# Column products with the high and low parts of the moving operand side by side, and a VectorE sum of the two halves

## The reference

```python
# first block
for i in (0, 1):
    mix = dsa_mixer(h, ...) if i == 0 else gla_mixer(h, ...)
    h = layer_norm(ALPHA * h + mix)
    h = layer_norm(ALPHA * h + square(relu(h @ w_up)) @ w_down)      # w_up 1024 x 4096
# second block
for i in (0, 1):
    mix = mla_mixer(h, ...) if i == 0 else hgrn2_mixer(h, ...)
    h = layer_norm(ALPHA * h + mix)
    gate, up = h @ w_in                                             # 1024 x 2 * 2816
    h = layer_norm(ALPHA * h + (silu(gate) * up) @ w_down)
    h = h + sigmoid(h @ w_ple_gate) * (p @ w_ple_proj)
```

## Time and profile before

| | |
|---|---|
| Median of 3 runs | 1422.44 us (1420.7 to 1422.44) |
| Profiled execution, its own time | 1421.68 us |
| Its span in the profile | 1419.9 us |
| TensorE busy with products | 1311.9 us (92%) |
| VectorE busy | 843.4 us (59%) |
| ScalarE busy | 572.2 us (40%) |
| Mean granted TensorE clock | 0.967 of full |

### The profile page before, as it was taken

How to read it: one execution, slowest core, us unless ns; L and a number is a source line. 1 busy time by engine, 2 the same in 40 slices (tenths; PEclk the granted TensorE clock), 3 DMA queues, 4 the chain that set the end, 5 groups by cost and what they waited for, 6 DMA issues and landing times.

```text
span 1419.9 us, 19097 instructions
## 1 busy us (share of the span) xinstructions
PE 1311.9 (92%) x8181; PEld 1185.4 (83%) x8181; DVE 843.4 (59%) x1146; ACT 572.2 (40%) x652; POOL 82.6 (6%) x198
## 2 busy tenths in 40 slices
PE   6978899997998899999878899999999988999997
PEld 5867799996987799997767899998898877999996
DVE  5584855557566755557645754447667658554465
ACT  5452344443633344443342433444451233433333
POOL 2450000000000000000230000000000000000000
PEclk9999999999999999999889999999999999999999
DMA  7410655554632455554330655555553325555542
GB/s 247 147 60 2 207 178 185 198 181 145 189 129 90 156 197 181 185 198 144 119 119 8 226 190 178 185 195 191 172 164 119 119 67 178 180 192 192 179 152 86
DMA packets 128757, 221.06 MB, mean 156 GB/s; under 512 B 6904, under 2 KB 97040, under 8 KB 128672
## 3 DMA queue, kind: packets, MB, share of 16 engines
q1 hardware_dynamic: 125648, 209.83, 44.1%
q0 software_dynamic: 3024, 10.01, 2.4%
HBM read 218.77 MB, written 1.05 MB: 155 GB/s over the span
## 4 chain that ended last, share of the span: by engine, by line
PE 80%; DVE 12%; ACT 4%; DMA 3%; issue 1%; POOL 0%; SPq 0%; ACTq 0%; POOLq 0%
PE ps L499 18%; PE ps L476 18%; PE ps L477 18%; PE ps L478 17%; PE ps L745 2%; DVE wlo L1354 2%; PE ps L584 2%; DVE y L1429 2%; DVE stats L1400 1%; PE ps L597 1%; DVE y L1397 1%; DVE x L1432 1%; ACT whi L1008 1%; ACT buf L1076 1%; PE ps L713 1%
## 5 line engine op out<-in xcount | busy, mean ns | idle before, releaser
L1354 DVE TENSOR_TENSOR wlo<-raw,whi 128x2048 fp32r<-128x2048 f32 (+2 forms) x201 | 454.0, 2265 | 259.1 <-ACT whi L1008 258.8
L1008 ACT ACTIVATE whi<-raw 128x2048 fp32r<-128x2048 f32 (+2 forms) x201 | 377.9, 1886 | 172.2 <-DMA raw<-in_mlp_w_down 46.5
L476 PE MATMUL ps<-xh,whi 128*128 128x256 f32 x1400 | 398.5, 285 | 6.1 <-ACT buf L1270 2.4
L477 PE MATMUL ps<-xh,wlo 128*128 128x256 f32 x1400 | 397.9, 284 | 0.0
L478 PE MATMUL ps<-xl,whi 128*128 128x256 f32 x1400 | 397.7, 284 | 0.0
L476 PEld LDWEIGHTS ps<-xh,whi 128*128 128x128 f32 x1400 | 270.3, 193 | 9.3 <-issue 5.0
L477 PEld LDWEIGHTS ps<-xh,wlo 128*128 128x128 f32 x1400 | 270.3, 193 | 1.6
L478 PEld LDWEIGHTS ps<-xl,whi 128*128 128x128 f32 x1400 | 270.2, 193 | 0.0
L476 PE MATMUL ps<-whi,hh 128*128 128x512 f32 x432 | 168.7, 390 | 0.0
L477 PE MATMUL ps<-whi,hl 128*128 128x512 f32 x432 | 168.6, 390 | 0.0
L478 PE MATMUL ps<-wlo,hh 128*128 128x512 f32 x432 | 168.1, 389 | 0.0
(11 more groups left out here) (281 smaller groups left out, 1101.8 us busy)
## 6 DMA issues: line engine op xcount, KB each, us to landing
raw<-in_ffn_w_in SPq DMA_DIRECT2D x44, 1024.0 KB, 5.1
raw<-in_mlp_w_up SPq DMA_DIRECT2D x32, 1024.0 KB, 5.4
raw<-in_mlp_w_down SPq DMA_DIRECT2D x32, 1024.0 KB, 4.9
raw<-in_ffn_w_down SPq DMA_DIRECT2D x22, 1024.0 KB, 4.8
raw<-in_hgrn_w_in SPq DMA_DIRECT2D x16, 1024.0 KB, 5.4
raw<-in_b_w_in SPq DMA_DIRECT2D x12, 1024.0 KB, 5.3
raw<-in_a_w_in SPq DMA_DIRECT2D x8, 1024.0 KB, 7.2
raw<-in_ple_w_gate SPq DMA_DIRECT2D x8, 1024.0 KB, 6.0
```

What stands on the lines that cost most here:

```text
L476: mm(o, a[0], b[0], start=start, stop=False)
L477: mm(o, a[1], b[0], start=False, stop=False)
L1008: a.activation(whi[:, slot, 0:w], raw[:, slot, 0:w], ACT.Copy).then_inc(s["hi_done"], 1)
L1354: v.tensor_tensor(wlo[:, slot, 0:w], raw[:, slot, 0:w], whi[:, slot, 0:w].bitcast(F32), ALU.subtract).then_inc(s["lo_done"], 1)
```

## The change

The parts `xh` and `xl` become the two halves of one tile `xhl` of [128 x 8 x 2 x 256]. A column chunk now uses two PSUM banks, one for each 128 features. For each of its 16 blocks the high weights multiply the high and low activations in one product of 512 columns, and the low weights multiply the high activations in one of 256 columns, which is added to the first half of the bank. VectorE then adds the two halves (`sum_parts`, a `tensor_reduce`, L1468) and writes the result to SBUF, from where ScalarE and VectorE go on. TensorE waits with a column chunk until the chunk two before it is summed. `turn_to_columns` waits for both parts of the whole operand before it starts.

```diff
-        xh = sb("xh", [P, KD, SEQ], F32R)
-        xl = sb("xl", [P, KD, SEQ], F32R)
+        xhl = sb("xhl", [P, KD, 2, SEQ], F32R)
+        xh, xl = xhl[:, :, 0, :], xhl[:, :, 1, :]
...
-            def columns(w, o, f0=0):
-
-                for f in range(f0, 2):
+            def columns(n, b):
+
+                k = column_no[n]
+                if k >= 2:
+                    pe.wait_ge(s["summed"], k - 1)
+                take(n)
+                w = weights(n, KD, FG)
+                for f in range(2):
                     for kk in range(KD):
-                        last = three(o[:, 256 * f : 256 * f + 256], [v[:, kk, P * f : P * f + P] for v in w],
-                                     [v[:, kk, :] for v in (xh, xl)], kk == 0, kk == KD - 1)
-                return last
-
-            def turn_to_columns(j, n, o):
+                        mm(bank(b + f), w[0][:, kk, P * f : P * f + P], xhl[:, kk, :, :].rearrange("p a n -> p (a n)"), start=(kk == 0), stop=False)
+                        last = mm(bank(b + f, 256), w[1][:, kk, P * f : P * f + P], xh[:, kk, :], start=False, stop=(kk == KD - 1))
+                last.then_inc(s["w_done"], 1)
+
+            def turn_to_columns(j, n, b):
 
                 for tt in range(TT):
                     turn_tile(j, x, tt)
-                take(n)
-                w = weights(n, KD, FG)
-                for step, (w_part, part) in enumerate(((0, 0), (1, 0), (0, 1))):
...
-                columns(w, o, 1).then_inc(s["w_done"], 1)
+                operand_ready(j, 1, 1, 1)
+                columns(n, b)
...
+            def sum_parts(n, b, dst):
+
+                dve.wait_ge(s["w_done"], n + 1)
+                v.tensor_reduce(dst, ps[:, b : b + 2, :].rearrange("p f (a n) -> p f n a", a=2), AX_X, ALU.add).then_inc(s["summed"], 1)
```

The engines that read the results change with it: in `mlp` VectorE sums, then does relu and square in one operation, and ScalarE only copies the high part; in `ffn` VectorE sums the gate and the up chunk; in GLA and HGRN the sums stand between the calls of `ahead`:

```diff
+            pe.wait_ge(s["summed"], column_no[first["gla_qk"] + 3] + 1)
...
             for q in range(4):
-                ahead(first["gla_qk"] + q)
+                n = first["gla_qk"] + q
+                ahead(n)
+                sum_parts(n, 2 * (q % 2), (q4[0] if q < 2 else k4[0])[:, 2 * (q % 2) : 2 * (q % 2) + 2, :])
...
             for q in range(2):
-                ahead(first["hgrn_f0"] + q)
+                summed_half("hgrn_f0", q, g4[0])
+            ahead(first["hgrn_q0"])
             gates(0)
             for q in range(2):
-                ahead(first["hgrn_q0"] + q)
+                summed_half("hgrn_q0", q, q4[0])
+            ahead(first["hgrn_f1"])
...
             for q in range(2):
-                ahead(first["hgrn_f1"] + q)
+                summed_half("hgrn_f1", q, g4[1])
             decay_steps(1, HGRN_EARLY[0])
+            ahead(first["hgrn_q1"])
             gates(1)
-            ahead(first["hgrn_q1"])
-            decay_steps(1, HGRN_EARLY[1])
-            ahead(first["hgrn_q1"] + 1)
-            decay_steps(1, HGRN_EARLY[2])
+            for q in range(2):
+                summed_half("hgrn_q1", q, q4[1])
+                decay_steps(1, HGRN_EARLY[1 + q])
```

More of the change, by code:

```diff
@@ L625, in mlp @@
                 dn = lambda g: first[f"down{layer}.{g}"]
-                turn_to_columns((T_X1, T_X3)[layer], up(0), bank(0))
+                turn_to_columns((T_X1, T_X3)[layer], up(0), 0)
                 def hidden(g):
-                    take(up(g))
-                    columns(weights(up(g), KD, FG), bank(4 + g % 3)).then_inc(s["w_done"], 1)
+                    columns(up(g), 4 + 2 * (g % 2))
                 for g in range(MLP_GROUPS - HOLD):
@@ L648, in ffn @@
                     for q in range(2):
-                        last = nc.tensor.transpose(ps[:, 1, 256 * q + P * tt : 256 * q + P * tt + P], ptok[:, tt, P * q : P * q + P], ident[:, :])
+                        last = nc.tensor.transpose(ps[:, 2, 256 * q + P * tt : 256 * q + P * tt + P], ptok[:, tt, P * q : P * q + P], ident[:, :])
                 last.then_inc(s["p_turned"], 1)
-                take(un(0))
-                columns(weights(un(0), KD, FG), bank(5)).then_inc(s["w_done"], 1)
+                columns(un(0), 6)
                 def hidden(g):
                     for w, n in enumerate((gn_(g), un(g))):
-                        take(n)
-                        columns(weights(n, KD, FG), bank(4 + 2 * (g % 2) + w)).then_inc(s["w_done"], 1)
+                        columns(n, 4 + 2 * w)
                 for g in range(FFN_GROUPS - HOLD):
@@ L852, in _ @@
             for q in range(4):
-                n = first["gla_qk"] + q
-                take(n)
-                columns(weights(n, KD, FG), bank(q)).then_inc(s["w_done"], 1)
+                columns(first["gla_qk"] + q, 2 * (q % 2))
                 if q == 0:
@@ L1205, in _ @@
                 ahead(n)
-                act.wait_ge(s["w_done"], n + 1)
-                dst = (q4[0] if q < 2 else k4[0])[:, 2 * (q % 2) : 2 * (q % 2) + 2, :].rearrange("p h n -> p (h n)")
-                a.activation(dst, bank(q), ACT.Copy, scale=float(P**-0.5) if q < 2 else 1.0).then_inc(s["qk_out"], 1)
+                act.wait_ge(s["summed"], column_no[n] + 1)
+                if q < 2:
+                    queries = q4[0][:, 2 * q : 2 * q + 2, :]
+                    a.activation(queries, queries, ACT.Copy, scale=float(P**-0.5)).then_inc(s["qk_out"], 1)
                 if q == 0:
@@ L1487, in mlp @@
                     ahead(up(g))
-                    dve.wait_ge(s["h_act"], hcount(layer, 0, g) + 1)
-                    v.tensor_tensor(full, r, r, ALU.mult).then_inc(s["h_full"], 1)
+                    sum_parts(up(g), 0 if g == 0 else 4 + 2 * (g % 2), two(r))
+                    dve.wait_ge(s["summed"], column_no[up(g)] + 1)
+                    v.scalar_tensor_tensor(full, r, 0.0, r, ALU.max, ALU.mult).then_inc(s["h_full"], 1)
                     dve.wait_ge(s["h_hi"], hcount(layer, 0, g) + 1)
@@ L1505, in ffn @@
                     ahead(gn_(g))
+                    sum_parts(gn_(g), 0 if g == 0 else 4, two(sig))
                     ahead(un(g))
```

78 lines of the change are left out of this document (38 added, 40 removed).

## The result

The changed kernel takes 1442.38 us (median of 4 runs, 1441.81 to 1443.20); the kernel before, on the same chip, 1422.44 us (4 runs, 1420.70 to 1422.90). The ratio is 1.0143, with a 95% interval of 1.0125 to 1.0160: slower by 19.9 us, where the prediction had 13.4 over its profiled execution and 1435.8 in all, with a range of 1427 to 1448. The profiled execution took 1442.2 us, its span is 1440.4 us (before 1419.9), its mean granted clock 0.957 (before 0.967).

The account below looks back on a forecast made before the run. TensorE, busy 92% of the span, was taken as the bound; -13.7 + 6.0 + 4.9 + 7.0 + 9.2 = +13.4 us on the profiled 1421.7 gave 1435.1, stated as a 1435.8 median, range 1427 to 1448.

Parts of the forecast that it names:

- Steady loops, -13.7: 72 column chunks outside GLA, HGRN and network starts: each 0.19 us cheaper on TensorE, 13.7 us saved.
- rival (a): Column chunks: mixed-length products save nothing, so the gain is near zero and the time 1449 us; chance 0.10.
- Stage starts, +6.0: Four mlp and ffn starts: TensorE waits for the last low part and full clock returns later, 1.5 us each.
- Ends, +4.9: Network ends: ScalarE and VectorE finish late, so the norm starts later, +2.0 for each silu network, +0.9 for one squared-relu.
- GLA, +7.0: GLA: ScalarE and VectorE wait for each other in a closed loop; v products +5.0 us later, plus 2.0 for half clock.
- the +2.0 for the clock: GLA: a half-clock stretch of about 4 us after TensorE's idling, costing 2.0 us, bounds 0 and 2.8.
- HGRN, +9.2: HGRN: the same closed loop, longer with gates ahead of two sums; v products start at 1086.1 instead of 1076.89.
- (b): VectorE's sum: dear, say 2.4 us, from reading PSUM with a stride; +16 us, so 1452 us; chance 0.09.
- (c): GLA, HGRN and ends: loops do not close, v products start no later than before; faster, 1412 us; chance 0.05.
- (d): Column chunks: a third fewer weight loads brings a chunk to its bare columns, 5.12 us; 1403 us; chance 0.03.

Follow-up runs that it names:

- the four orders: Changed kernel with sums ahead of weight rounding (GLA, HGRN), no low-part wait in first chunks, products grouped by length, ScalarE's high part before its last copy: 1410.85, again 1409.36 us.
- the grouped kernel: Changed kernel with eight 512-column products, then eight 256-column ones, in each block of 128 features instead of alternating pairs: 1442.90 us, ratio 1.0151.
- The run with the sums first: Changed kernel with VectorE's sums ahead of the next chunk's weight rounding in GLA and HGRN, and no ScalarE wait for GLA's k sums: 1430.02 us, ratio 1.0063.
- the reordered kernels: Changed kernel with VectorE summing before it rounds the next weights in GLA and HGRN: 1430.02 us; with three further orders altered too, 1410.85 us.
- the early start: Changed kernel with the first half of a stage's first column chunk in old-order 256-column products, waiting for the last low part last: 1439.15 us, ratio 1.0108.

## Why the prediction was right, and what was off in it

The sign, the mechanism and the range were right. The main step, that orders of work on ScalarE and VectorE eat the gain on TensorE, is shown from both sides. The start wait alone, put into the kernel before, costs 10.6 us; the four orders changed in the new kernel turn +1.4% into -1.0%. The sizes were less sure: the loss was 19.9 us and not 13.4, because the gain came out at half its size and the starts and ends cost more, while HGRN and the rest made up for 3.1 of it.

**Steady loops, -13.7: mis-sized.** Measured are 64 chunks for -6.6 us, and 8 more at the starts, some -7.4 together. The step that was off was to add the two pitches of the earlier trace rows, 0.228 and 0.1198, each of which was taken from a run of products of one length. In the alternating order a pair takes 0.353 and not 0.348; the grouped kernel, with 5.56 us a chunk, shows that the sum of the pitches is right where lengths don't alternate. (Another 0.3 us is rounding: 5.75 - 5.565 is 0.185 a chunk, and the forecast took 0.19.) So rival (a), that the mixing eats the gain, came true for nearly half of it (6.6 of 12.2 us came). The formula of the Trainium skill's page "TensorE: Matmul & The Clock Gate", section "Back-to-back issue gap", which the section gives for a product taken by itself, would have a pair at 0.325 us in either order; the traces of both orders disagree, 0.353 and 0.348.

**Stage starts, +6.0: too small.** They cost 7.5 us with 8 cheaper chunks inside, about 8.3 without them, or 2.1 each. The wait was 1.41 us, near the 1.6 said. What I took too low is the half clock: after the later start it lasted 4.9 us; I took a value near the 3.05 us of before (3.2 by the clock of the finer windows), and named the longer one, 5 us or +2.4, as the upper bound. It came out near that bound. The wait in the kernel before says the same, 2.3 us a start.

**Ends, +4.9: 6.5 measured.** The norm itself came 1.5 us later, less than the 2.0. In the segments behind the two `ffn` it is 3.1 and 2.9. The rest is half clock behind the norm, which the forecast left out: from 1000 to 1005 us the granted clock was 0.75, and before it was full from there to HGRN's start.

**GLA, +7.0: 6.9 measured.** The loop is the one forecast, but the near match of the total is partly luck. Up to v it is +4.46 against +5.0, once the stage's own later start (0.7 us) is taken off; the +2.0 for the clock was 2.4, and the two errors cancel. The order of VectorE is shown to be the cause by the run that alters only that.

**HGRN, +9.2: 7.6 measured.** The waits stand where they were forecast, ahead of the third pair (3.76 us) and behind the decay step (2.49). The chain of some 25 steps was 1.6 us too long. The run with the sums first gave 6.5 of it back.

**The rivals.** (b) fell: the sum is 1.221 us. (c), loops that don't close, is what the reordered kernels are; it is true of them and not of the change. (d) fell: a chunk is 5.64 us, with a third of the weight loads gone.

**What stays open.** Waits and clock are not independent, and single edits don't add up: 19.4 us apart, 33.0 together; the grouping gives nothing alone and 9.8 us with the others. (Against the kernel before of each comparison the gap is wider still, 14.0 and 32.8. Each single edit is known only to within 3 to 5 us, so the size of the gap is uncertain.) In the traces the gains are where the theory puts them, and with single edits they are then partly gone in segments of unchanged code. There the clock goes with it. Time at half clock is twice the missing share of the mean clock times the span: about 94 us before, 124 in the changed kernel, 126 with the early start, 158 in the grouped execution, 90 with all four. So the changed kernel has 30 us more at half clock, and the four orders take that away. What makes a half-clock stretch come or stay away in code that is the same is not settled by these runs. Nor did any run give the kernel before a new order in HGRN, so a part of the last kernel's lead may be open to it as well.

## What to carry to other kernels

A helper engine with slack in its busy share can still close a loop with another: look at the order on both engines wherever an instruction is added, and put what frees a bank or feeds the other engine ahead of work for a later chunk. Take the pitch of a product from the order in which it will run, not from runs of one length, and group by length where it can be done. Merging operands also merges their waits: a product of high and low parts side by side can start only when the later one is there, and here those 1.4 us cost 2.2 to 2.7 with the clock behind them (the four starts of the two runs that alter the wait alone). A change that loses is worth taking apart before it is dropped: this one loses 1.4% as written, and gains 1.0% with four orders altered around it.

## What was not expected of the hardware

- Alternating 512- and 256-column products cost 0.353 us a pair; grouped by eights, a pair costs 0.348 (5.64 and 5.56 us a chunk, divided by its 16 pairs).
- A reduction of 128x1024 values out of PSUM, with its two halves 256 values apart, takes 1.221 us, as long as a reduction of 1024 neighbouring values in SBUF (1.220). A copy of half as many takes 0.690.
- The same instructions from 120 to 140 us ran at a mean granted clock of 1.00 in one execution and 0.66 in another, which moved all behind it by 5.2 us; 0.66 came back in the slowest runs of two more kernels. So one span alone can mislead by that much here; the same segment in two traces, and several runs, tell more.
